# High and low activations side by side in one 512-column product for the 336 projection blocks with features on partitions

## The reference, cut to what matters

```
def nsa_mixer(x, w_in, w_out, shared):
    proj = x @ w_in
    q = proj[..., :ATTN_WIDTH] ...
    z = proj[..., ATTN_WIDTH:ATTN_WIDTH * (1 + N_BRANCH)] ...
    o = jnp.stack(nsa_attention(q, *shared), axis=2)
    y = jnp.sum(gate[..., None] * o * jax.nn.silu(z), axis=2)
    return y @ w_out
...
def swiglu_ffn(h, w_in, w_out):
    g, u = jnp.split(h @ w_in, 2, axis=-1)
    return (jax.nn.silu(g) * u) @ w_out
```

## Time and profile before

| | |
|---|---|
| median of 3 runs | 3943.48 us (3941.76 to 3947.19) |
| the profiled execution: its time | 3947.24 us |
| its span, first to last instruction | 3945.5 us |
| mean granted clock of TensorE | 0.967 of full speed |
| PE busy | 3680.2 us, 93% of the span |
| DVE busy | 2140.2 us, 54% |
| ACT busy | 1617.5 us, 41% |
| DMA | 612 MB, 155 GB/s mean |

### The profile page before, as it was taken

The page is one execution under the profiler, slowest core; times in us unless marked ns, Lnnn a source line. Parts: engine busy times, 40 slices in busy tenths (PEclk is TensorE's granted clock), DMA queues, the critical chain, the costliest instruction groups (busy, mean ns, idle before and its releaser), DMA issues.

```text
span 3945.5 us, 60283 instructions
## 1 busy us (share of the span) xinstructions
PE 3680.2 (93%) x24695; PEld 3366.3 (85%) x24695; DVE 2140.2 (54%) x2737; ACT 1617.5 (41%) x2144; POOL 241.6 (6%) x232
## 2 busy tenths in 40 slices
PE   7888799999997999989999999999989899999998
PEld 6766799999977997768989989899777699899897
DVE  5887634555656545555444444554555554444444
ACT  4334323655643333444433333343333354333333
POOL 3562000000000020000000000000000000000000
PEclk9988899999998999989999999999998899999999
DMA  7324456555454564435656656555324356566564
GB/s 207 97 86 145 136 150 181 140 151 149 139 192 124 175 160 128 150 107 149 175 183 184 182 186 180 184 164 160 124 90 135 101 159 181 181 181 181 182 185 144
DMA packets 859333, 612.34 MB, mean 155 GB/s; under 512 B 10370, under 2 KB 752305, under 8 KB 858144
## 3 DMA queue, kind: packets, MB, share of 16 engines
q1 hardware_dynamic: 857072, 602.21, 52.3%
q0 software_dynamic: 2096, 7.81, 0.7%
HBM read 607.82 MB, written 2.16 MB: 155 GB/s over the span
## 4 chain that ended last, share of the span: by engine, by line
PE 83%; DVE 9%; ACT 3%; issue 2%; POOL 2%; DMA 0%; ACTq 0%; DVEq 0%; SPq 0%
PE acc L897 48%; PE acc L887 27%; PE psC L990 2%; DVE wL L1658 2%; PE psA L959 1%; ACT wH L1256 1%; DVE xtok L1619 1%; PE psC L945 1%; DVE arena L1965 1%; PE psB L945 1%; PE psB L973 1%; ACT L1256 1%; POOL arena L760 0%; PE psA L862 0%; DMA xtok<-in_x 0%
## 5 line engine op out<-in xcount | busy, mean ns | idle before, releaser
L1658 DVE TENSOR_TENSOR wL<-ring,wH 128x1024 fp32r<-128x1024 f32 x1128 | 1336.4, 1226 | 1125.3 <-ACT wH L1256 1120.6
L897 PE MATMUL acc<-actH,wH 128*128 128x256 f32 x5760 | 1654.8, 287 | 28.4 <-DVE wL L1658 28.4
L897 PE MATMUL acc<-actL,wH 128*128 128x256 f32 x5760 | 1632.4, 283 | 0.0
L897 PE MATMUL acc<-actH,wL 128*128 128x256 f32 x5760 | 1632.1, 283 | 0.0
L1256 ACT CAST wH<-ring 128x1024 fp32r<-128x1024 f32 x1128 | 1125.1, 1046 | 1223.2 <-PE acc L887 631.9
L897 PEld LDWEIGHTS acc<-actH,wH 128*128 128x128 f32 x5760 | 1108.3, 192 | 40.7 <-DVE wL L1658 23.0
L897 PEld LDWEIGHTS acc<-actL,wH 128*128 128x128 f32 x5760 | 1108.3, 192 | 4.8 <-issue 3.3
L897 PEld LDWEIGHTS acc<-actH,wL 128*128 128x128 f32 x5760 | 1107.7, 192 | 0.0
L887 PE MATMUL acc<-wH,actH 128*128 128x512 f32 x896 | 365.5, 408 | 25.9 <-DVE actL L1650 22.8
L887 PE MATMUL acc<-wL,actH 128*128 128x512 f32 x896 | 356.6, 398 | 0.0
L887 PE MATMUL acc<-wH,actL 128*128 128x512 f32 x896 | 355.7, 397 | 0.0
(11 more groups left out here) (294 smaller groups left out, 2488.1 us busy)
## 6 DMA issues: line engine op xcount, KB each, us to landing
ring<-in_w_ffn_in SPq DMA_DIRECT2D x176, 1024.0 KB, 5.7
ring<-in_w_ffn_out SPq DMA_DIRECT2D x88, 1024.0 KB, 5.1
ring<-in_b_w_in SPq DMA_DIRECT2D x64, 1024.0 KB, 6.2
ring<-in_w_in_ab SPq DMA_DIRECT2D x56, 1024.0 KB, 5.5
ring<-in_w_in_c SPq DMA_DIRECT2D x48, 1024.0 KB, 5.7
ring<-in_kv_w SPq DMA_DIRECT2D x24, 1024.0 KB, 5.6
ring<-in_a_w_in SPq DMA_DIRECT2D x16, 1024.0 KB, 7.1
ring<-in_w_xkv SPq DMA_DIRECT2D x16, 1024.0 KB, 5.7
```

Source lines behind the costliest of these rows:

```text
L897: ins = pe.matmul(dst, w[:, t, f * P:(f + 1) * P], x[:, t, :], start=t == 0 and n == 0, stop=t == ph.kt - 1 and n == 2)
L1658: dve.tensor_tensor(wL[:, split_slot, cols], ring[:, slot, cols], wH[:, split_slot, cols].bitcast(F32), ALU.subtract).then_inc(l_made, 1)
```

## The change

For every feat projection but three early ones (`s5_u`, `s5_z` and the memory keys, with `s5_glu`) the high and the low activations lie side by side (`act2`), and the high weights multiply both in one product of 512 columns. The left 256 columns of the bank then hold high by high, the right 256 low by high, and the third product, high by low, is added to the right half. A block has 32 products instead of 48 and fills a whole bank; it streams 768 columns for each feature tile, as before. The two halves must be added at the end of a chunk: ACT copies the left halves of both blocks out (`take_left`, one copy of 512), then DVE adds the right halves from PSUM (`add_right`). For the gate projections ACT takes the silu afterwards, in place, from SBUF, behind the first block's split of the next chunk (`silu_chunk`); at the last chunk of a projection it stands ahead of the next projection's first split.

```diff
+        act2 = sb("act2", P, FT, 2, T, dt=F32R)
+        actH, actL = act2[:, :, 0, :], act2[:, :, 1, :]
...
+        def take_left(act, ph, i, c, dst):
+            act.wait_ge(blocks_done, ph.blocks_before(i, c, ph.blocks))
+            first = 2 * ph.pair(c)
+            act.copy(dst, acc[:, first:first + 2, 0:T]).then_inc(left_out, 1)
+        def add_right(dve, ph, i, c, dst, left):
+            dve.wait_ge(left_out, ph.lefts(i, c))
+            first = 2 * ph.pair(c)
+            return dve.tensor_tensor(dst, left, acc[:, first:first + 2, T:2 * T], ALU.add)
...
+                elif ph.joined:
+                    bank = pair[:, b, :]
+                    for t in range(ph.kt):
+                        if turn_call is not None and c == 0 and b == 0:
+                            pe.wait_ge(turned_l, FT * turn_call + t + 1)
+                        pe.matmul(bank.rearrange("p (h t) -> p h t", h=2), high[:, t, :], act2[:, t, :, :],
+                                  start=t == 0, stop=False)
+                        ins = pe.matmul(bank[:, T:2 * T], low[:, t, :], xH[:, t, :], start=False,
+                                        stop=t == ph.kt - 1)
...
+            def silu_chunk(ph, dst, n):
+                await_chunk(act, ph, n)
+                z = dst[:, 2 * n:2 * n + 2, :]
+                act.activation(z, z, ACT.Silu).then_inc(z_silu, 1)
+            def z_steps(ph, dst, k=None):
+                chunks = ph.iters * ph.body
+                for n in range(chunks):
+                    for b in range(ph.blocks):
+                        if b == ph.blocks - 1 and k is not None:
+                            z_free(k, 2 * n)
+                        one_block(ph, n // ph.body, n % ph.body, b, dst)
+                        if b == 0 and n >= 1:
+                            silu_chunk(ph, dst, n - 1)
+                        yield
+                silu_chunk(ph, dst, chunks - 1)
...
                         if c == 0:
                             wait_past(act, drained[ffn_in.pair(1)], ffn_in.pair_uses(i, 1))
-                            act.activation(silu_g, src, ACT.Silu).then_inc(drained[ffn_in.pair(0)], 1)
+                            take_left(act, ffn_in, i, 0, silu_g)
                         else:
+                            act.wait_ge(drained[ffn_in.pair(0)], ffn_in.pair_uses(i, 0) + 1)
+                            act.activation(silu_g, silu_g, ACT.Silu).then_inc(silu_done, 1)
+                            take_left(act, ffn_in, i, 1, up_left)
                             act.wait_ge(drained[ffn_in.pair(1)], ffn_in.pair_uses(i, 1) + 1)
...
                         if u["fin"] == "gate":
-                            await_chunk(dve, *u["output_after"])
+                            dve.wait_ge(z_silu, u["z_chunk"] + 1)
...
+                            if c == 0:
+                                add_right(dve, ffn_in, i, 0, silu_g, silu_g).then_inc(drained[ffn_in.pair(0)], 1)
+                        add_right(dve, ffn_in, i, 1, hid_f, up_left).then_inc(up_summed, 1)
+                        dve.wait_ge(silu_done, i + (pairs_done + 1))
+                        dve.wait_ge(up_summed, i + (pairs_done + 1))
+                        dve.tensor_tensor(hid_f, hid_f, silu_g, ALU.mult).then_inc(drained[ffn_in.pair(1)], 1)
```

More of the change, by code:

```diff
@@ L347, in program @@
         out_done = sem("out_done")
-        plan = {"blocks": 0, "chunks": 0}
+        plan = {"blocks": 0, "chunks": 0, "joined": 0}
         def columns(w, kt, cols):
@@ L354, in columns, with feat @@
             return lambda j, k=0: v[:, k * kt:(k + 1) * kt, bass.ts(j, cols)]
[L356 removed]
+        def feat(w, first, tiles, iters=1, joined=True):
             at = columns(w, FT, P)
@@ L1480, in _, with z_free @@
-            alternate(attend(nsa_units), join(*(
-                [block_steps(b_z[0][r], silu_z(r)) for r in range(BRANCHES)] + [block_steps(b_q[1])] +
-                [block_steps(b_z[1][r], silu_z(BRANCHES + r)) for r in range(BRANCHES)])), nsa_counts)
+            dense(kv[1])
+            dense(kv[2], kwT)
+            dense(kv[3])
+            dense(b_q[0], qT)
+            def z_free(k, tile):
+                if k > 0:
+                    hh, r = divmod(k - 1, BRANCHES)
+                    if r == 0:
+                        act.wait_ge(o_used, nsa[hh][0][tile + 1]["group"] + 1)
+                    else:
+                        act.wait_ge(branch_summed, NH * hh + 8 * (r - 1) + tile + 2)
@@ L1483, in _ @@
+            blocks = join(*(
+                [z_steps(b_z[0][r], zT, r) for r in range(BRANCHES)] + [block_steps(b_q[1], qT)] +
+                [z_steps(b_z[1][r], zT, BRANCHES + r) for r in range(BRANCHES)]))
+            alternate(attend(nsa_units), blocks, nsa_counts)
+            for _ in blocks:
+                pass
             act.wait_ge(branch_summed, 2 * NH)
@@ L1495, in decays @@
                     act.activation(table[:, h, :], table[:, h, :], ACT.Exp).then_inc(decay_ready, 1)
-            dense(ab_rq)
-            alternate(decays(), block_steps(ab_rk), [1] * 8)
+            dense(ab_rq, rqT)
+            alternate(decays(), block_steps(ab_rk, rkT), [1] * 8)
             dense(ab_rv)
-            blocks = join(block_steps(ab_nq), block_steps(ab_nk), block_steps(ab_nv))
+            blocks = join(block_steps(ab_nq, nqT), block_steps(ab_nk, nkT), block_steps(ab_nv))
             for _ in range(8):
@@ L1506, in _ @@
                 next(blocks)
-            alternate(attend(na), block_steps(ab_rg, lambda i, c, src: act.activation(
-                rgT[:, bass.ds(i * 4 + 2 * c, 2), :], src, ACT.Silu)), [1] * 8)
+            blocks = z_steps(ab_rg, rgT)
+            alternate(attend(na), blocks, [1] * 8)
+            for _ in blocks:
+                pass
             act.wait_ge(gated, 1)
@@ L1553, in _ @@
             turn_out(TURN_MIX[1], G_MIX + 16)
-            dense(c_q)
-            blocks = join(block_steps(c_k), block_steps(c_v))
+            dense(c_q, dqT)
+            blocks = join(block_steps(c_k, dkT), block_steps(c_v))
             alternate(head_roots(norm_c), blocks, [2] * 8 + [1] * 4)
@@ L1665, in one_block @@
                     split_weights(n % SLOTS, n % SPLIT_SLOTS, ph.blocks_before(i, c, b) + 1)
-                if b == ph.blocks - 1 and fn is not None:
+                if b == ph.blocks - 1 and ph.joined:
+                    dst = feat_slot(ph, fn, i, c)
+                    add_right(dve, ph, i, c, dst, dst).then_inc(drained[ph.pair(c)], 1)
+                elif b == ph.blocks - 1 and fn is not None:
                     drain_chunk(dve, ph, i, c, fn)
```

76 lines of the change are left out of this document (33 added, 43 removed).

## The result

The changed kernel takes 4075.2 us (median of four runs, 4056.4 to 4082.1) against 3942.6 for the kernel before: ratio 1.0327, 95% interval 1.0291 to 1.0363. It is slower, as forecast, but by 132 us, where the forecast had 55 and its range ended at 4030.

What follows compares the result with a forecast made beforehand. TensorE in the two block loops, 75% of the span, was taken to bound the kernel. Five terms, -10.9, +3.4, +42.5, +4.9 and +15.3, summed to +55 us: 3998.6 us, 1.4% slower, range 3965 to 4030.

Steps and rivals of the forecast that it cites:

- TensorE-alone blocks: 64 blocks with only TensorE on the path: 0.21 us saved each, less four later stage ends; -10.9 us.
- head norm steps: 32 blocks save 6.7 us, but 16 chunk drains move 0.63 us later ahead of the spread product; +3.4 us.
- sparse attention: Later gate multiplies, b_q[1] drains and silu at projection changes outweigh 24 blocks' savings; +42.5 us.
- neighbourhood attention: Copy L1792 1.0 us later for three chunks, plus 1.9 for silu and table load at the end; +4.9 us.
- feed-forward: 44 passes of four blocks: multiply and all behind it come 1.3 us later, partly offset by faster blocks; +15.3 us.
- the silu ahead of the cast: Sparse attention, five changes of projection: table load and silu delay a cast by 1.9 us each; +9.5 us.
- the wait for `wL` in the feed-forward: Parts two and three: `wL` ends at 6.5 us but is wanted at 5.55, late by 0.97 each pass.
- 1: Rival: nothing is paid at the gate multiply and in the feed-forward pass; 3883 us, chance 0.05.
- 2: Rival: the feed-forward pass has more room, its 176 blocks gain 37 us and lose nothing; about 3946 us, chance 0.05.
- 3: Rival: a 512-column and a 256-column product in turn cost 0.360 us, no saving; 4052 us, chance 0.05.
- How the numbers follow: Step setting the range from unknowns in copy, handover, waiting steps and product pair: 3965 to 4030 us, chance 0.85.
- the pair of products: A 512-column and a 256-column product in turn taken as 0.347 us; 0.353 instead would add 26 us.

Runs made afterwards that it cites:

- e4: Changed kernel with both drains of b_z and ab_rg chunks held back one attention step and each projection's last silu behind the next's first cast: 4013.5 us.
- e5: Changed kernel with only the silu of a projection's last chunk moved behind the next projection's first cast: 4063.5 us.
- e3: Changed kernel with the feed-forward's end of pass moved behind the next pass's first weight split, gate half's drains behind the following split: 4010.0 us.
- e1: Changed kernel with its drains kept but each 512-column product split again into two of 256: 4121.8 us.
- e14: Kernel before the change with three spare DVE additions ahead of the multiply at the end of each feed-forward pass: 4041.8 us.
- e13: Kernel before the change with one spare DVE addition ahead of the multiply at the end of each feed-forward pass: 3965.0 us.
- e2: Changed kernel with all sixteen 512-column products of a block ahead of its sixteen 256-column ones: 4066.5 us.

## Why the prediction was wrong in size

By its own terms, for the profiled execution. The change is from block start to block start; "clock" is half the additional time at half clock in the same stretch, "rest" is what the terms speak of.

| term | forecast | change | clock | rest |
|---|---|---|---|---|
| TensorE-alone blocks | -10.9 | -8.0 | +0.2 | -8.2 |
| head norm steps | +3.4 | +12.5 | +8.5 | +4.0 |
| sparse attention | +42.5 | +53.2 | +12.3 | +40.9 |
| neighbourhood attention | +4.9 | +2.5 | +1.1 | +1.4 |
| feed-forward | +15.3 | +49.2 | +25.5 | +23.7 |
| the rest | 0 | 0.0 | -1.7 | +1.7 |
| sum | +55 | +109 | +46 | +63 |

- **Right**: the order of the drains and its price. The gate multiply at 1.55, the product at 2.11, +1.30 in a 256-key step, two-block steps of 14.95 us for "near 14.8", the silu ahead of the cast, the wait for `wL` in the feed-forward: all stand in the rows above where the prediction put them, and e4, e5 and e3 take them away by moving the drains alone. Of the rivals, 1 and 2 are refuted by the waits themselves, 3 by the blocks of 5.55 and 5.65 us. Its 0.97 us for the wait is 0.95 by its own figures (6.5 less 5.55), which changes nothing.
- **The step that failed** is "How the numbers follow". Its unknowns were handovers, one more step that waits, and the pair of products; the clock was taken as that of the kernel before, in which no feed-forward pass behind another has a stretch at half clock. The changed kernel has 24 more short half-clock stretches, and its clock time in the profiled run is 46 us greater. That its new waits bring most of this is shown where moving the drains removes both: all of the 12 us in the sparse attention (e4), some 19 of the 25 in the feed-forward (e3). The trace of before had the warning, at the ends of the feed-forward's parts, where waits of 2.6 to 2.9 us had a stretch behind them in three of six places. The median lies another 23 us further off (132.6 against 109.2, each against its kernel before), at a lower clock, most of it probably the 34 us stretch behind `kv_cmp`. Together that is 69 of the 77 us missed. The range of 3965 to 4030 could not hold it, since none of its cases let the clock move.
- **A term mis-sized**: the feed-forward, 23.7 for 15.3. The pair of products in turn takes 0.353 us in most blocks, not 0.347. The prediction named that as worth up to 26 us and chose the lower bound, because loads lie under products at both widths; the rows that it had showed each width by itself, not the turn. A pass of parts two and three has a wait of 0.82 us (forecast 0.97); 7 of the 24 take the 23.2 us forecast, but in 17 most blocks take 5.65, and these take 23.5. The same 0.3 us stands in part one between passes of 24.63 and of 24.95.
- **Neighbourhood attention** came out 3.5 us cheaper than forecast. I did not follow that up.

## What to carry to other kernels

An operation that is added behind a product costs by what is queued behind it on its engine: a copy and an addition of 0.6 to 0.7 us cost 1.3 to 1.6 us a step with the addition ahead of the gate multiply and nothing in the hole behind the maximum, so look for the hole first. A wait that a change adds on TensorE has a second price, when it is long enough to lower the clock: look for waits of that size in the trace before and at the clock behind them, and put the range's end there. When an edit saves less than its blocks show, compare the granted clock before looking for another mechanism.

## What the runs showed of the hardware

- After a wait of TensorE of 2.2 us in otherwise dense work the clock was at 1.2 GHz for 3.4 us in 8 of 14 passes, after 2.1 us in 11 of 14 of e1, and after 2.6 us in 12 of 14 of e14; after 0.8, 1.2 and 1.4 us in none. Each such stretch costs 1.5 to 1.6 us. After waits of 2.6 to 2.9 us at the ends of the feed-forward's parts it was so in 3 of 6 (the kernel before); after 3.2 to 3.6 (e13), 4.0 to 4.3 (the changed kernel) and 4.4 to 4.8 us (e14) in 6 of 6 each, for 3.4 or 6.8 us.
- A 512-column and a 256-column product in turn take 0.347 us in some blocks and 0.353 in others, of the same code at a granted clock of 1.00: the two undisturbed passes above, 24.63 and 24.95 us, differ by that. With all wide ones first (e2) they take 0.348, where no wait falls into the block. Why a block falls to one or the other is open.
